# Adding the experts' output bias inside the first combination instead of ahead of the first down projection, in a single-core decoder step on Trainium2

## The reference

```python
def expert_ffn(xb, w_gu, b_gu, w_d, b_d):
    gu = xb @ w_gu + b_gu
    gate, up = jnp.split(gu, 2, axis=-1)
    gate = jnp.minimum(gate, SWIGLU_LIMIT)
    up = jnp.clip(up, -SWIGLU_LIMIT, SWIGLU_LIMIT)
    glu = gate * jax.nn.sigmoid(SWIGLU_ALPHA * gate)
    return ((up + 1) * glu) @ w_d + b_d
...
    y = jnp.einsum('nk,nkd->nd', gates.astype(y_sel.dtype), y_sel)
```

## Time and profile before

| | us |
|---|---|
| median of 3 runs | 1318.89 |
| lowest, highest | 1316.85, 1319.54 |
| the profiled execution | 1318.1 |
| its span, first to last instruction | 1316.5 |
| PE busy in it | 1178.7 |
| DVE busy in it | 322.2 |

### The profile page before, as it was taken

How to read it: one execution, slowest core, us unless ns; L and a number is a source line. 1 busy time by engine, 2 the same in 40 slices (tenths; PEclk the granted TensorE clock), 3 DMA queues, 4 the chain that set the end, 5 groups by cost and what they waited for, 6 DMA issues and landing times.

```text
span 1316.5 us, 15247 instructions
## 1 busy us (share of the span) xinstructions
PE 1178.7 (90%) x5966; PEld 600.4 (46%) x5966; DVE 322.2 (24%) x582; ACT 174.3 (13%) x343; POOL 48.3 (4%) x95
## 2 busy tenths in 40 slices
PE   5999998999999989898898979797988979797987
PEld 2788755788643434434242424244342424243433
DVE  2379865333222011102101110111021011101142
ACT  2132231100210200100020002001000200020002
POOL 0121231000000000000000000000000000000000
PEclk9999999999898999998999999999999999999998
DMA  9998999975679999999999999999999999999991
GB/s 353 350 351 306 379 323 338 401 309 188 261 322 415 409 414 419 416 417 418 416 421 414 422 414 422 415 420 417 417 419 415 421 414 422 414 421 409 419 414 72
DMA packets 106350, 500.50 MB, mean 380 GB/s; under 512 B 8762, under 2 KB 10920, under 8 KB 70849
## 3 DMA queue, kind: packets, MB, share of 16 engines
q1 hardware_dynamic: 99456, 478.38, 90.6%
q0 software_dynamic: 6576, 21.42, 4.6%
q10 hardware_dynamic: 272, 0.09, 0.0%
HBM read 496.48 MB, written 3.38 MB: 380 GB/s over the span
## 4 chain that ended last, share of the span: by engine, by line
PE 69%; DMA 24%; DVE 2%; ACT 2%; issue 2%; SPq 1%; DVEq 0%
PE ps L957 26%; DMA ring<-in_w_d 21%; PE ps L460 11%; PE ps L1021 10%; PE ps L1123 4%; PE ps L897 3%; PE ps L823 2%; PE ps L778 2%; DMA ring<-in_w_ada 2%; PE ps L394 2%; DMA ring<-in_w_gu 1%; PE ps L425 1%; PE ps L847 1%; PE ps L634 1%; PE ps L913 1%
## 5 line engine op out<-in xcount | busy, mean ns | idle before, releaser
L957 PE MATMUL ps<-ring,zone 128*64 128x512 f32 x2000 | 439.4, 594 | 22.5 <-DMA ring<-in_w_gu 20.6
L1021 PE MATMUL ps<-ring,oT 128*64 128x512 f32 x1024 | 246.8, 639 | 66.0 <-DMA ring<-in_w_d 66.0
L957 PEld LDWEIGHTS ps<-ring,zone 128*64 128x64 f32 x2000 | 143.1, 137 | 314.8 <-issue 298.8
L1021 PEld LDWEIGHTS ps<-ring,oT 128*64 128x64 f32 x1024 | 87.2, 147 | 224.4 <-issue 224.4
L1953 DVE TENSOR_SCALAR zone<-ps 128x1024 f32<-128x1024 f32 x16 | 19.6, 1225 | 595.9 <-PE ps L957 595.9
L460 PE MATMUL ps<-hT,ring 128*128 128x264 f32 x640 | 149.2, 391 | 2.1 <-DVE hT L1540 1.8
L460 PEld LDWEIGHTS ps<-hT,ring 128*128 128x128 f32 x640 | 121.0, 192 | 28.5 <-issue 7.4
L1390 ACT ACTIVATE attn<-zone 128x1024 f32<-128x1024 f32 x16 | 16.9, 1056 | 464.1 <-DVE zone L1953 464.1
L1970 DVE TENSOR_TENSOR zone<-zone,ps 128x264 f32<-128x264 f32 x56 | 24.0, 429 | 147.2 <-PE ps L1123 147.2
L394 PE MATMUL ps<-ident,zone 128*128 128x128 f32 (+3 forms) x212 | 32.9, 283 | 20.4 <-DMA zone<-in_b_alpha 10.6
L897 PE MATMUL ps<-zone,tok 128*128 128x224 f32 x224 | 44.2, 356 | 0.1
(11 more groups left out here) (375 smaller groups left out, 785.7 us busy)
## 6 DMA issues: line engine op xcount, KB each, us to landing
ring<-in_w_gu SPq DMA_DIRECT2D x123, 2048.0 KB, 17.5
ring<-in_w_d SPq DMA_DIRECT2D x62, 2048.0 KB, 17.7
ring<-in_w_ada SPq DMA_DIRECT2D x12, 2048.0 KB, 12.6
ring<-in_w_in SPq DMA_DIRECT2D x9, 2048.0 KB, 13.8
ring<-in_cache_k SPq DMA_DIRECT2D x32, 256.0 KB, 7.0
ring<-in_cache_k POOLq DMA_DIRECT2D x32, 256.0 KB, 6.4
ring<-in_cache_v SPq DMA_DIRECT2D x32, 256.0 KB, 9.7
ring<-in_cache_v POOLq DMA_DIRECT2D x32, 256.0 KB, 8.3
```

The costliest lines, as they stand in the source:

```text
L957: ins = pe.matmul(ps[64 * j:64 * j + CAP, c, :], xg[:, k, 2 * par + j, :], rows, start=False, stop=(k == KT - 1), skip_group_check=True)
L1021: ins = pe.matmul(ps[64 * j:64 * j + CAP, 4 + c, :], hidT[:, k, j * CAP:(j + 1) * CAP], w[j][:, kk, c * 512:(c + 1) * 512], start=(k == 0) ...
```

## The change

The bias is no longer computed in the first quad. `combine` takes a flag `biased`; with it, each block m gets the bias product as the first of three that add up in the same bank. That is the combination of q = 0, which stands in the quad q = 1, so this quad is written out on TensorE ahead of the loop, which now runs over q = 2 to 6. VectorE still copies the turned gates to `gatesT`, and now clears `acc` with a memset where it copied. Its own loop is as it was. The counts of the semaphore `added` fall by eight.

```diff
-            def output_bias():
-                pe.wait_ge(sig("b_d"), 16)
-                pe.wait_ge(sig("gatesT"), 1)
-                for m in range(KT):
-                    if m >= 2:
-                        pe.wait_ge(sig("added"), m - 1)
-                    else:
-                        pe.wait_ge(sig("read"), 5 + m)
-                    pe.matmul(ps[:, 6 + m % 2, 0:T], b_d_sb[:, m * P:(m + 1) * P], gatesT,
-                              start=True, stop=True).then_inc(sig("summed"), 1)
...
-            def combine(q):
-
+            def combine(q, biased):
+
+                if biased:
+                    pe.wait_ge(sig("b_d"), 16)
+                    pe.wait_ge(sig("gatesT"), 1)
                 pe.wait_ge(sig("ye_ready"), q * 2 + 2)
                 pe.wait_ge(sig("read"), q * 10 + 10)
                 for m in range(KT):
                     if m >= 2:
-                        pe.wait_ge(sig("added"), q * KT + (KT + m - 1))
+                        pe.wait_ge(sig("added"), q * KT + (m - 1))
                     else:
                         pe.wait_ge(sig("read"), q * 10 + (15 + m))
+                    if biased:
+                        pe.matmul(ps[:, 6 + m % 2, 0:T], b_d_sb[:, m * P:(m + 1) * P], gatesT, start=True, stop=False)
                     for par in range(2):
                         ins = pe.matmul(ps[:, 6 + m % 2, 0:T], ye_tok[par][:, m * P:(m + 1) * P], putT[:, par, :],
-                                        start=(par == 0), stop=(par == 1))
+                                        start=(par == 0 and not biased), stop=(par == 1))
                     ins.then_inc(sig("summed"), 1)
...
                     turn_hidden(q, 0, cold, first)
-                    if cold:
-                        output_bias()
                 else:
                     down(q - 1, 1, False, False)
                     turn_hidden(q, 0, cold, first)
-                    combine(q - 1)
+                    combine(q - 1, biased)
                     gate_up(q, 1, False, False)
+                if cold:
+                    pe.wait_ge(sig("gatesT"), 1)
                 down(q, 0, False, cold)
...
                 quad(q, True, cold)
-                with pe.Fori(1, QUADS - 1) as i:
+                if cold:
+                    quad(q + 1, False, False, biased=True)
+                with pe.Fori(2 if cold else 1, QUADS - 1) as i:
                     quad(q + i, False, False)
...
                 if cold:
-                    output_bias()
+                    dve.wait_ge(sig("gates_turned"), 1)
+                    V.tensor_copy(gatesT, ps[0:NE, 4, 0:T]).then_inc(sig("gatesT"), 1)
+                    chain(V.memset(acc, 0.0))
                 swiglu(q, 1, False, q * 10 + 6 if first else None)
...
-            def output_bias():
-
-                dve.wait_ge(sig("gates_turned"), 1)
-                V.tensor_copy(gatesT, ps[0:NE, 4, 0:T]).then_inc(sig("gatesT"), 1)
-                for m in range(KT):
-                    dve.wait_ge(sig("summed"), m + 1)
-                    V.tensor_copy(acc[:, m, :], ps[:, 6 + m % 2, 0:T]).then_inc(sig("added"), 1)
-                dve.wait_ge(sig("added"), KT)
```

More of the change, by code:

```diff
@@ L978, in turn_hidden @@
                         pe.wait_ge(sig("read"), q * 10 + (3 + 2 * par + g))
-                    if par == 1:
-                        pe.wait_ge(sig("added"), q * KT + (7 + g))
+                    if par == 1 and not cold:
+                        pe.wait_ge(sig("added"), q * KT + (g - 1))
                     for k in range(4):
@@ L989, in turn_put @@
                     if last:
-                        pe.wait_ge(sig("added"), q * KT + (par - 1 + KT))
+                        pe.wait_ge(sig("added"), q * KT + (par - 1))
                     else:
@@ L1068, in final_turns @@
                         if t == 0 and k % 2 == 0:
-                            pe.wait_ge(sig("added"), q * KT + (KT + m + 2))
+                            pe.wait_ge(sig("added"), q * KT + (m + 2))
                         ins = transpose(ps[:, Y_BANKS[2 * g + t], k * P:(k + 1) * P],
@@ L1096, in last_quad @@
                 turn_hidden(q, 0, False, False)
-                combine(q - 1)
+                combine(q - 1, False)
                 down(q, 0, True, False)
@@ L1118, in combine, with quad @@
                     if m >= 2:
-                        pe.wait_ge(sig("added"), q * KT + (KT + m - 1))
+                        pe.wait_ge(sig("added"), q * KT + (m - 1))
                     else:
                         pe.wait_ge(sig("read"), q * 10 + (15 + m))
+                    if biased:
+                        pe.matmul(ps[:, 6 + m % 2, 0:T], b_d_sb[:, m * P:(m + 1) * P], gatesT, start=True, stop=False)
                     for par in range(2):
                         ins = pe.matmul(ps[:, 6 + m % 2, 0:T], ye_tok[par][:, m * P:(m + 1) * P], putT[:, par, :],
-                                        start=(par == 0), stop=(par == 1))
+                                        start=(par == 0 and not biased), stop=(par == 1))
                     ins.then_inc(sig("summed"), 1)
-            def quad(q, first, cold):
+            def quad(q, first, cold, biased=False):
                 gate_up(q, 0, first, cold)
@@ L1139, in quad @@
                     turn_hidden(q, 0, cold, first)
-                    combine(q - 1)
+                    combine(q - 1, biased)
                     gate_up(q, 1, False, False)
+                if cold:
+                    pe.wait_ge(sig("gatesT"), 1)
                 down(q, 0, False, cold)
-                turn_hidden(q, 1, cold, first and not cold)
+                turn_hidden(q, 1, cold, first)
                 turn_put(q)
@@ L1150, in one_round @@
                 if not cold:
-                    pe.wait_ge(sig("added"), q * KT + KT)
+                    pe.wait_ge(sig("added"), q * KT)
                     pe.wait_ge(sig("x2_samples"), rnd)
@@ L1968, in add_quad @@
                 for m in range(KT):
-                    dve.wait_ge(sig("summed"), q * KT + (KT + m + 1))
+                    dve.wait_ge(sig("summed"), q * KT + (m + 1))
                     V.tensor_tensor(acc[:, m, :], acc[:, m, :], ps[:, 6 + m % 2, 0:T], ALU.add)\
@@ L2033, in finish @@
                     if m % 2 == 0:
-                        dve.wait_ge(sig("summed"), q * KT + (KT + m + 2))
+                        dve.wait_ge(sig("summed"), q * KT + (m + 2))
                     V.scalar_tensor_tensor(out=xT[:, m, 0:TP], in0=ps[:, m // 2, (m % 2) * TP:(m % 2 + 1) * TP],
```

## The result

The changed kernel took 1328.10 us (median of 4 runs, 1326.37 to 1328.73) against 1319.07 for the kernel before beside it (4 runs, 1316.85 to 1319.54). The two medians are 9.0 us apart; the ratio of times on record is 1.0051, smaller than that of these medians (1.0068), with a 95% interval of 1.0030 to 1.0073. On another occasion (8 runs against 31) the ratio was 1.0045, 1.0027 to 1.0064, and the medians were 1326.89 and 1321.03 us, 5.9 apart. It is slower, by some 6 us or more, where 1320.1 was forecast, with an upper end of 1322.6.

What follows compares the result with a forecast made beforehand. The weight stream was taken as the bound from some 395 us on. The profiled execution plus the four parts, 1318.1 + 0 + 0 + 0.8 + 1.2, gave 1320.1 us, range 1317.0 to 1322.6.

Steps and rivals of the forecast that it cites:

- part 3: Eight bias products in combine(0): 3.7 us more on TensorE, next issue at 512.3, stream loses 0.8 us once.
- rival C: Bias products cost 6.3 us in combine, queue runs dry for 3.4 us; 1322.7 us; chance 0.14.
- the rule of the later of (landing + 5.0) and (issue + 7.5): First load of a pair lands at the later of landing ahead plus 5.0 us and issue plus 7.5 us.
- part 1: Bias block leaves its place ahead of down(0, 0): 6.3 us off TensorE, 0 off the stream.
- rival B: With TensorE earlier, the pair of 449.8 is issued in time, 1.1 us of transfer returns; 1317.0 us; chance 0.20.
- Rival D: The bias block was on the chain and its 6.3 us are won whole; 1311.8 us; chance 0.06.
- Part 2: Clearing acc on VectorE by a 1.9 us memset in place of eight copies: 0.
- Part 4: Second turn written out ahead of TensorE's loop: 0 for its work, 1.2 us for its code.
- my sign that 545 to 665 us would be longer than two steady periods: If 545 to 665 us were no longer than a steady pair of periods, the code's 1.2 us would be wrong.

Runs made afterwards that it cites:

- 128 rows: Changed kernel with bias and turned gates padded with zero rows, so the eight bias products are 128 rows high; 1.0018 of the kernel before.
- twice the bias: Changed kernel with each bias product in combine(0) done twice; 1.0066 of the kernel before.
- old block with q = 1 out: Kernel before, bias block in its old place, with only q = 1 written out ahead of TensorE's loop; 1.0001 of the kernel before.
- kernel without bias: Changed kernel without the eight bias products and with q = 1 back in the loop; 0.9984 of the kernel before.
- bias between down's halves: Kernel before with its bias block moved between the halves of down(0, 0); 1.0007 of the kernel before.
- without bias and q = 1 out: Changed kernel without the eight bias products, q = 1 still written out ahead of the loop; 1.0016 of the kernel before.
- changed kernel again: The changed kernel, unaltered, timed and profiled once more; 1.0045 of the kernel before.
- half the bias: Changed kernel with bias products for only the first four of the eight blocks; 1.0018 of the kernel before.
- bias in down: Bias as first term of each expert's down, four products a pair, bias block gone, q = 1 in the loop; 1.0052 of the kernel before.

## Why the prediction was wrong

**The step that failed is part 3, "Eight bias products in combine(0): 3.7 us on TensorE, 0.8 us on the stream".** It is a term of the sum, and the mechanism in it, a late issue into a queue that has run dry, is the one that the runs show. Its size was off twice. What came is rival C, to which I gave 0.14, and more of it than its 1322.7 us.

*0.231 us a pass, 3.7 us.* It measured 6.45 us (13.84 - 7.39). I priced the bias product by the passes of combine, as if only columns counted. The block's own row gave 6.2 us for eight, and I put that down to its waits for VectorE's copies; that the two prices nearly agree is partly luck, since the block ran partly at 1.2 GHz (with less of that it took 5.2 us, above), while in combine the change of height came on top. With 128 rows the price is what I had reckoned, 3.5 us.

*0.8 us on the stream.* Relative to a period of 60.2 it measured 5.0. Rival C, with my own rule and 6.3 us, gave 3.4 for it, and 3.5 is what the first landing lost: the rule of the later of (landing + 5.0) and (issue + 7.5) held, with 7.3 to 7.8 us in the dry spells. But the first landing is not the whole loss. The empty queue left 4.5 us of transfer undone, and the period grew by 5.0. The measure that fails is the landing time of the first load; the missing bytes, which I had worked out for the spot at 450 us and set aside in part 1 ("The landing does not show it"), are the one to go by. With the right price for the products the term would still have been too small: 128 rows high, with 3.5 us of growth, they cost the stream 2.1 us and not 0.8, since only 1.4 us of growth are free and not 2.9.

What the first landing does not show comes out at a later one. In the changed kernel the w_d loads land at 538.4, 543.6 (the first pair), 550.1 and 555.2 us, so the third comes 6.5 us behind the second, where 5.1 to 5.6 are usual. The first dry spell of the kernel before, at 388 us, has the like: its third and fourth w_d loads land at 416.9 and 423.1, 6.2 apart. With twice the bias it is the first w_d load, 6.3 us behind the load ahead. Why that load and not the one before it stays open.

**Part 1** was right in the main: no 6.3 us gain, a wait to the landing near 423 (429.7 here, with the start 6.7 later), a lower clock behind it. TensorE entered gate_up(1, 0) 0.6 us earlier (93.1 against 93.7), less than the 1.0 to 2.2 worked out, since the half behind the wait took 8.5 to 8.8 us. The first period fell from 135.1 to 134.4 us where I had 0. That the missing transfer at 450 us, rival B's 1.1 us, can come back is shown: the first period follows the lead. That it is the change that brought it is not, since the old block with q = 1 out has 134.4 too. Rival D falls by the kernel without bias.

**Part 2** was right: clearing acc cost nothing that shows.

**Part 4**, 1.2 us for the doubled code: not borne out. The old block with q = 1 written out is at 1.0001. Its written-out turn cost nothing over 60.2, and an excess of 1.4 us stood in the loop's first turn, a pair of periods later. Nor is the excess a fixed price of that turn: it was 0.4 to 0.5 us in the kernel before and in the one without bias in the loop, 0.9 to 1.1 in the changed one, and nothing in the one with the bias between down's halves (60.27), in the one with twice the bias and in the one without bias and q = 1 out. So my sign that 545 to 665 us would be longer than two steady periods came true in the changed kernel (its third and fourth periods are 61.05 + 60.47 = 121.5 us, two steady ones 120.4), but by another cause. There the down half behind the late wait took 9.32 us at the lower clock and not 7.11 (555.37 in the chain), the next issues came later, and the rate fell to 289 GB/s in 582 to 585 us, 0.9 us of transfer missing. The changed kernel again, 128 rows and half the bias have the same (8.7 to 8.8 us); with twice the bias the half took 7.11, and nothing is missing. What the 1.4 us of the old block with q = 1 out are stays open; that it was the fetches was a guess of mine. Of the Trainium skill, "Runtime: NRT & Kernel Launch", Instruction fetch mechanics, the sentence that crossing a block is mostly hidden agrees with this (five blocks in 540 to 700 us, and 1.0001) better than my 1.2 us did.

**The base.** I summed upon one execution of 1318.1 us. Its start at 348.97 was one of the lucky ones, and in the later comparisons the kernel before had medians of 1319.90 to 1321.03. The changed kernel's profiled execution, at 1328.73, is 10.6 us above it: 6.7 of that lie ahead of the expert part and 3.8 in it. Its medians are 10.0 and 8.8 us above. 4.8 of each are the stream's loss; the kernel before was itself 1.0 and 2.9 us above its profiled execution in these two comparisons; the remaining 4.2 and 1.1 us stay open. The range had no term for the base.

## What to carry to other kernels

Work that is free on a waiting engine is free only up to the point where it delays the issue that refills a queue: find for each place the distance between that issue and the last landing ahead of it, take off the latency from an empty queue and a microsecond or more, since the queue thins out before it is empty (1.4 us were free here, where the rule of the first landing gave 2.9), and compare that with the work, at a price that the same shape has in the trace. Price a dip by the bytes that it does not carry, and not by how late its first load lands. When one spot of the program has a row for exactly the moved operation, that row is the price until an experiment shows why it should be another. And compare stages from a common mark, not whole executions, when what lies ahead of the mark differs by more than the change.

## What was not expected of the hardware

A product of 32 rows and 264 columns among products of 128 rows cost 0.64 us and made the two behind it 0.20 us longer; padded with zeros to 128 rows it cost 0.45 us and they kept their 0.89. A second low product right behind the first cost only 0.44 us: the change of height costs, not the height.

Products of 32 rows, with 64 columns of weights and 512 columns, took a time that goes with how many of them lie on one strip of 32 rows. Eight on four strips, two on each, took 1.04 us (L847 ahead of each gate_up). Four on two strips, two on each, took 1.02 us at 2.4 GHz, as in the changed kernel again:

```profile
341.24 1.02 PE ps L847 x8
```

Four on one strip took 1.93 us (L999). So products on different strips appear to run side by side, and the bias in down would have been cheaper on four strips; that was not tried.
